# A hybrid two-layer block on one core: front, second norm, mixer's bias, first delta-rule head's preparation and end rewritten around unchanged heads

## The reference, cut to what matters

```
for i in range(2):
    shift, scale, gate = split(silu(c) @ ada_w[i] + ada_b[i])        # c_shift, c_scale, c_gate from c_ctx
    h  = rms_norm(x,   norm_w[i]) * (1 + scale)   + shift             # x: 256 latent tokens, ctx: 256 context tokens
    hc = rms_norm(ctx, norm_w[i]) * (1 + c_scale) + c_shift           # width 2048
    if i == 0:   # mixer: spatial gate  u * (w_s @ layernorm(v) + b_s) * silu(ga)  in 8 groups,
                 # and attention with 8 heads, 2 key/value heads, rms-normed and rotated q, k
        o, oc = ab_mixer(h, hc, ...)
    else:        # q, k, v through a 5-tap convolution and silu, 16 key heads x 2 value heads, gated delta rule
                 # in both directions (chunks), output rms-normed, times silu(z), then @ w_out
        o, oc = dn_mixer(h, hc, ...)          # only the latent part of the output is needed
    x = x + gate * o
    if i == 0: ctx = ctx + c_gate * oc
return rms_norm(x, final_norm_w)
```

## Time and profile before

| what | us |
|---|---|
| median of 3 runs (2880.4 to 2884.49) | 2881.23 |
| the profiled execution, its own time | 2878.12 |
| its span, first to last instruction | 2876.3 |
| PE busy in it (92%) | 2650.1 |
| DVE, ACT, POOL busy | 1219.5, 1233.4, 1287.2 |
| mean granted clock of TensorE, share of full speed | 0.964 |

### The profile page before, as it was taken

How to read it: one execution, slowest core, us unless ns; L and a number is a source line. 1 busy time by engine, 2 the same in 40 slices (tenths; PEclk the granted TensorE clock), 3 DMA queues, 4 the chain that set the end, 5 groups by cost and what they waited for, 6 DMA issues and landing times.

```text
span 2876.3 us, 58157 instructions
## 1 busy us (share of the span) xinstructions
PE 2650.1 (92%) x24892; PEld 2223.1 (77%) x24892; DVE 1219.5 (42%) x2427; ACT 1233.4 (43%) x2210; POOL 1287.2 (45%) x780
## 2 busy tenths in 40 slices
PE   4699999999999665999999999999999999997898
PEld 0277777777778454888888888888888888886897
DVE  0212222222310322565565555655655566554323
ACT  2422333333322324465456545654565456443333
POOL 2032333333245524544554555455545554551353
PEclk8899999999999877999999999999999999998999
DMA  6835444455442202213222322232222222214554
GB/s 277 330 108 185 186 174 174 183 190 190 161 176 88 73 30 91 74 61 104 89 76 67 104 82 82 68 101 85 78 71 97 89 74 75 97 53 147 183 184 132
DMA packets 98897, 351.54 MB, mean 122 GB/s; under 512 B 10833, under 2 KB 15313, under 8 KB 96210
## 3 DMA queue, kind: packets, MB, share of 16 engines
q1 hardware_dynamic: 98642, 347.82, 34.3%
HBM read 335.59 MB, written 12.19 MB: 121 GB/s over the span
## 4 chain that ended last, share of the span: by engine, by line
PE 72%; POOL 12%; issue 6%; DVE 3%; DMA 3%; ACT 3%; SPq 0%; POOLq 0%; ACTq 0%; DVEq 0%
PE bank L522 8%; PE bank L524 7%; PE bank L523 7%; PE bank L684 4%; PE bank L686 4%; PE bank L685 4%; POOL wl L385 3%; PE bank L790 3%; PE bank L498 3%; POOL scratch L2059 2%; DMA raw<-w_ada 2%; PE bank L724 2%; PE bank L808 2%; PE bank L726 2%; PE bank L725 2%
## 5 line engine op out<-in xcount | busy, mean ns | idle before, releaser
L385 POOL TENSOR_TENSOR wl<-raw,wh 128x1024 fp32r<-128x1024 f32 x210 | 500.3, 2386 | 722.3 <-ACT wh L380 722.3
L380 ACT ACTIVATE wh<-raw 128x1024 fp32r<-128x1024 f32 x226 | 238.7, 1059 | 548.5 <-PE bank L686 258.4
L684 PE MATMUL bank<-hh,wh 128*128 128x512 f32 (+1 forms) x1040 | 410.6, 395 | 49.7 <-POOL wl L385 24.8
L686 PE MATMUL bank<-hh,wl 128*128 128x512 f32 (+1 forms) x1040 | 387.4, 372 | 0.9 <-issue 0.9
L685 PE MATMUL bank<-hl,wh 128*128 128x512 f32 (+1 forms) x1040 | 385.8, 371 | 1.3 <-issue 1.3
L684 PEld LDWEIGHTS bank<-hh,wh 128*128 128x128 f32 x1040 | 201.7, 194 | 86.1 <-POOL wl L385 25.9
L522 PE MATMUL bank<-hh,wh 128*128 128x512 f32 x640 | 256.8, 401 | 11.8 <-POOL wl L328 11.8
L328 POOL TENSOR_TENSOR wl<-raw,wh 128x1024 fp32r<-128x1024 f32 x56 | 136.7, 2446 | 254.7 <-ACT wh L323 254.7
L524 PE MATMUL bank<-hh,wl 128*128 128x512 f32 x640 | 250.4, 391 | 0.0
L523 PE MATMUL bank<-hl,wh 128*128 128x512 f32 x640 | 250.2, 391 | 0.0
L686 PEld LDWEIGHTS bank<-hh,wl 128*128 128x128 f32 x1040 | 201.3, 194 | 35.9 <-issue 1.7
(11 more groups left out here) (277 smaller groups left out, 5995.6 us busy)
## 6 DMA issues: line engine op xcount, KB each, us to landing
raw<-w_in SPq DMA_DIRECT2D x258, 512.0 KB, 3.5
raw<-w_ada SPq DMA_DIRECT2D x124, 512.0 KB, 6.5
raw<-w_out SPq DMA_DIRECT2D x84, 512.0 KB, 3.8
scratch<-w_ada SPq DMA_DIRECT2D x68, 512.0 KB, 6.3
scratch<-keep_g SPq DMA_DIRECT2D x16, 1024.0 KB, 6.0
scratch<-w_in SPq DMA_DIRECT2D x24, 512.0 KB, 7.0
scratch<-xT SPq DMA_DIRECT2D x2, 4096.0 KB, 12.8
keep_y<-scratch SPq DMA_DIRECT2D x30, 256.0 KB, 2.4
```

The source lines that it names most:

```text
L380: eng.activation(buffers(s)[0], raw[:, s % RAW, :], ACT.Copy).then_inc(sem("rear_hi"), 1)
L385: eng.tensor_tensor(buffers(s)[1], raw[:, s % RAW, :], buffers(s)[0].bitcast(F32), ALU.subtract)\
L684: pe.matmul(ps, w[:, k * P:(k + 1) * P], hhv[:, kk, t0:t1], start=first and k == k0, stop=False)
L686: done = pe.matmul(ps, r[:, k * P:(k + 1) * P], hhv[:, kk, t0:t1], start=False, stop=last and k == k1 - 1)
```

## The change

Six parts; the numbers are used again further on.

1. Front: the squares 0 to 9 come ahead of the rows of block 0 and 10 to 15 behind them; `square_sum(0)` comes after three units of block 2; a read-out of rows stands behind every second `norm_affine`; the first halves of key tiles 0 and 1 are loaded after block 5 and multiplied inside blocks 6 and 7; half 2 is loaded after block 6, and its split stands behind `norm_affine(11)`.
2. Mixer: the bias is loaded on all partitions and added by DVE; the matmul of ones goes.
3. Second norm: eight buffers of each kind instead of two.
4. Head 0: sums of the decay rows come in the middle of the key tile, later weight halves are split between the steps, two of the four coupling tiles and both attention tiles go from POOL to DVE, the second value tile's convolution goes behind `turn_first`.
5. Last head: the first two output halves are multiplied in four quarters between steps of the scan, for which y of heads 0 to 7 must be back (counted on `g_kept`).
6. Last norm: the product with `final_w` is made on ACT beside the output tiles, the product with the root is shared by DVE (10 tiles) and POOL (6), and 8 stores of two tiles replace 16.

```
+SOONER = {5: (0, 1), 6: (2,)}
@@ order of the ring (front_places), and the same on SP
     for a in range(len(EARLY)):
         eighths(a, 0, 8)
-    for h in range(4 * KVH):
+        for h in SOONER.get(a, ()):
+            half(h)
+    for h in range(3, 4 * KVH):
         half(h)
+        def norm_t(layer, k):
+            return xres[:, k % 8, :] if layer else n_t[k % 2]
+        def norm_full(layer, k):
+            return xres[:, 8 + k % 8, :] if layer else n_full[k % 2]
@@ SP
-            sp.dma_start(sgub[0:1, :], sgu_b).then_inc(sem("mix_in"), 16)
+            sp.dma_start(sgub, sgu_b[0:1, :].to_broadcast([P, GROUPS * P])).then_inc(sem("mix_in"), 16)
...
+                back = sem("g_kept" if h < KH // 2 else "y_back")
...
@@ PE, front
-                ada(a, 3, 8, pb[2 + a % 2])
-                if a == 1:
+                if a == 2:
                     square_sum(0)
+                ada(a, 3, 5, pb[2 + a % 2])
+                if a >= NEARLY - 2:
+                    front_half(a - NEARLY + 2, pb[a - NEARLY + 2][:, :], True, False, "h_lo", 0)
+                ada(a, 5, 8, pb[2 + a % 2])
...
-            kv_tile(0)
-            kv_tile(1)
+            front_half(2, pb[0][:, :], False, True, "h_lo", 1)
+            front_half(3, pb[1][:, :], False, True, None, 1)
@@ PE, mixer
-                pe.matmul(pb[5][:, :].rearrange("p (t n) -> p t n", n=P), ones[0:1, :], rep, start=True, stop=False)
@@ PE, head 0 (k and q quarters stood ahead of the sums, turn_k, make_kk, make_kq behind both v tiles)
+            k_quarter(0, 0, pb[4])
+            k_quarter(0, 1, pb[4])
             pe.wait_ge(sem("g_ready"), 1)
...
+            k_quarter(0, 2, pb[4])
             pe.wait_ge(sem("gc_ready"), 1)
...
+            v_quarter(0, 0, 0, pb[6])
+            turn_k(0)
+            v_quarter(0, 0, 1, pb[6])
+            make_kk(0)
+            v_quarter(0, 0, 2, pb[6])
+            make_kq(0)
+            v_quarter(0, 0, 3, pb[6])
@@ PE, last head
                 scan_su(i, 1)
                 if more:
                     z_eighth(i, 1, PB)
+                else:
+                    out_quarter(0)
...
@@ ACT, head 0
             for t in range(NT):
                 decay_distance(0, t)
-            decay(0)
+                decay(0, t, t + 1)
+                if t == 0:
+                    rear_split_hi(act, 9)
+            rear_split_hi(act, 10)
@@ DVE, mixer
-                dve.tensor_tensor(xv[:, n, :], pb[5][:, :], a_ug, ALU.mult).then_inc(sem("a_merged"), 1)
+                ch.link(dve.tensor_tensor(xv[:, n, :].rearrange("p (t n) -> p t n", n=P),
+                                          pb[5][:, :].rearrange("p (t n) -> p t n", n=P), rep, ALU.add))
+                dve.tensor_tensor(xv[:, n, :], xv[:, n, :], a_ug, ALU.mult).then_inc(sem("a_merged"), 1)
@@ DVE, head 0 (new)
+            for t in (2, 3):
+                dve.wait_ge(sem("e_exp"), t + 1)
+                dve.tensor_tensor(q4(attn[0][t - 2]), q4(CT(0, t)), each_v(KQM[:, 2 * (t - 2) * P:2 * (t - 1) * P]),
+                                  ALU.mult).then_inc(sem("at_ready"), 1)
+                ch.link(dve.tensor_tensor(q4(CT(0, t)), q4(CT(0, t)), each_v(KKM[:, 2 * t * P:2 * (t + 1) * P]),
+                                          ALU.mult))
+                dve.tensor_tensor(u4(CT(0, t)), u4(CT(0, t)), coef(0, 0, t), ALU.mult).then_inc(sem("c_ready"), 1)
             for g in range(2):
                 turn_first(0, g)
+            conv_v(0, 1, pb[7], 0, 5)
@@ end
+                act.activation(f_out[:, t, :], x1[:, t, :], ACT.Copy, scale=smc("final_w")[:, t:t + 1])
-            for k in range(KT):
-                dve.scalar_tensor_tensor(out=f_out[:, k, :], in0=x1[:, k, :], scalar=smc("final_w")[:, k:k + 1],
-                                         in1=f_rinv, op0=ALU.mult, op1=ALU.mult).then_inc(sem("f_scaled"), 1)
+            for k in range(10):
+                dve.tensor_tensor(f_out[:, k, :], f_out[:, k, :], f_rinv, ALU.mult).then_inc(sem("f_scaled"), 1)
+            for k in range(10, KT):                                   # on POOL
+                pool.tensor_tensor(f_out[:, k, :], f_out[:, k, :], f_rinv, ALU.mult).then_inc(sem("n_added"), 1)
```

More of the change, by code:

```diff
@@ L482, in _, with store @@
                 rear_load(sp, s, w_out1[s - NDELTA, :, :])
-            for k in range(KT):
-                sp.wait_ge(sem("f_scaled"), k + 1)
-                sp.dma_start(out[k, :, :], f_out[:, k, :]).then_inc(sem("stored"), 16)
-            sp.wait_ge(sem("stored"), 16 * KT)
+            pairs = out.rearrange("k p t -> p k t")
+            def store(j):
+                sp.dma_start(pairs[:, 2 * j:2 * j + 2, :], f_out[:, 2 * j:2 * j + 2, :]).then_inc(sem("stored"), 16)
+            for j in range(5):
+                sp.wait_ge(sem("f_scaled"), 2 * j + 2)
+                store(j)
+                if j in (1, 2, 4):
+                    p = (1, 2, 4).index(j)
+                    sp.wait_ge(sem("n_added"), 3 * (KT - 1) + 2 * p + 2)
+                    store(5 + p)
+            sp.wait_ge(sem("stored"), 16 * KT // 2)
         @block.tensor
@@ L512, in square_sum, with front_half @@
                 pe.matmul(pb[6][:, :], ones[:, :], n_acc, start=True, stop=True).then_inc(sem("n_summed"), 1)
-            def front_half(h, ps, first, last, ready=None):
+            def front_half(h, ps, first, last, ready=None, part=None):
                 pe.wait_ge(sem("front_lo"), h + 1)
@@ L892, in scan_su, with out_quarter @@
                 done.then_inc(sem("su_made"), 1)
+            def out_quarter(q):
+                s = NDELTA + q // 2
+                if q == 0:
+                    pe.wait_ge(sem("z_silu"), KH)
+                    pe.wait_ge(sem("g_kept"), 16 * 2 * NT + 32 * (KH // 2))
+                if q % 2 == 0:
+                    wait_lo(pe, s)
+                w, r = buffers(s)
+                for k in range(4 * (q % 2), 4 * (q % 2) + 4):
+                    kk = (q // 2) * HALF + k
+                    ps = PA[:, 0:SEG]
+                    pe.matmul(ps, w[:, k * P:(k + 1) * P], hhy[:, kk, :], start=(kk == 0), stop=False)
+                    pe.matmul(ps, w[:, k * P:(k + 1) * P], hly[:, kk, :], start=False, stop=False)
+                    done = pe.matmul(ps, r[:, k * P:(k + 1) * P], hhy[:, kk, :], start=False, stop=False)
+                if q % 2:
+                    done.then_inc(sem("rear_done"), 1)
             def query_s(i, t):
@@ L917, in _ @@
             products(1, 0, HALF, PA[:, :], 0, T, False, True, "h_lo")
-            for q in range(4):
-                k_quarter(0, q, pb[4])
             pe.wait_ge(sem("ba_copied"), 1)
@@ L923, in _ @@
             done.then_inc(sem("ba_turned"), 1)
-            for q in range(4):
-                q_quarter(0, q, pb[5])
+            k_quarter(0, 0, pb[4])
+            k_quarter(0, 1, pb[4])
             pe.wait_ge(sem("g_ready"), 1)
@@ L933, in _ @@
             done.then_inc(sem("g_summed"), 1)
-            for q in range(4):
-                v_quarter(0, 0, q, pb[6])
+            k_quarter(0, 2, pb[4])
             pe.wait_ge(sem("gc_ready"), 1)
@@ L1063, in _ @@
                     pe.wait_ge(sem("x2_ready"), t - 1)
-                for j in range(4):
+                for j in range(2 if t == 0 else 0, 4):
                     s = NDELTA + 4 * t + j
@@ L1156, in k_root @@
                    .then_inc(sem("k_root"), 1)
-            for h in range(4):
-                front_split_hi(act, h)
+            front_split_hi(act, 4)
             kv_copy(0)
             k_square(0)
-            front_split_hi(act, 4)
             front_split_hi(act, 5)
@@ L1288, in _ @@
                .then_inc(sem("gexp"), 1)
[L1289 to L1294 removed]
+            rear_split_hi(act, 5)
             def decay_distance(h, t):
@@ L1303, in decay_distance, with decay @@
                 last.then_inc(sem("e_min"), 1)
-            def decay(h):
-                for t in range(NT):
+            def decay(h, t0=0, t1=NT):
+                for t in range(t0, t1):
                     act.wait_ge(sem("e_min"), 4 * h + t + 1)
@@ L1953, in _ @@
                 scan_s(i, 0)
+                if not more:
+                    rear_split_lo(dve, NDELTA + 1)
                 scan_r(i, 1)
@@ L2116, in _ @@
                 add_final(k)
+            pool.wait_ge(sem("n_scaled"), 2 * KT + 1)
+            for k in range(10, KT):
+                pool.tensor_tensor(f_out[:, k, :], f_out[:, k, :], f_rinv, ALU.mult).then_inc(sem("n_added"), 1)
 def halves(w):
@@ L2200 @@
     tiles0 = [32, 33, 34, 35] + [t for g in range(GROUPS) for t in (24 + g, 8 + g, g, 16 + g, 36 + g)]
-    h0 = h0[[2 * t + b for t in tiles0 for b in range(2)]]
+    order0 = [2 * t + b for t in tiles0 for b in range(2)]
+    order0[1:3] = order0[2:0:-1]
+    h0 = h0[order0]
     w1 = np.asarray(dn_w_in[0])
```

155 lines of the change are left out of this document (87 added, 68 removed).

## The result

| | us |
|---|---|
| before, median of 4 runs (2880.4 to 2884.49) | 2882.09 |
| changed, median of 4 runs (2789.84 to 2798.23) | 2794.07 |
| ratio, 95% interval | 0.9694, [0.9676, 0.9712] |
| the changed kernel's profiled execution: its time, its span | 2791.92, 2790.1 |
| predicted | 2793.0, range 2775 to 2811 |

The kernel is 88.0 us faster. That the total was met to 1 us says little yet, since it is a sum of six terms. The two profiled executions have spans 86.2 us apart, and seven instructions that stand in both cut them into eight stretches. The first two groups are rows of the changed kernel's timeline, one engine at a time (columns as in the earlier trace rows).

A forecast was written before the change was run, and what follows sets the result against it. PE was taken as the limit in mixer and heads, standing still in edited places; DVE and POOL limit the second norm. 33 + 8.4 + 1.5 + 49 - 4.7 + 1 = 88.2 us off 2881.23 gives 2793, range 2775 to 2811.

The forecast's parts named there:

- six slots hold 7.7 us of loads, so PE's absence alone costs DMA little: Front: an early half takes 6.2 us of PE, which the loads in six slots were to cover.
- single stall of half 2: Front: half 2's slot comes free only when split, behind two more norm tiles, putting the end of block 7 at 108.
- a sign of being wrong: Front: the prediction is wrong if the first norm's ACT queue holds back the ring for longer than one half.
- Rival (a): Second norm: DVE and POOL run free of the lock, 14 us off instead of 1.5, total 2780; chance 0.13.
- the 3 kept back: Head 0: 3 us kept from 51.8 for unseen waits, POOL's two first subtractions and ACT's wait for the late convolution.
- POOL's two subtractions as late work: Head 0: POOL now begins with two subtractions, 4.8 us, that used to be done, covered by the 3 us kept.
- the clock should rise earlier: ... less 0.9 for one step: Last scan: one step at the upper clock, 1.13 against 2.08 us, takes 0.9 us off the quarters' cost.
- rival (c): Last scan: filled gaps keep the clock up, five slow steps gain 4.7 us, cancelling part 5, total 2788; chance 0.12.
- 7.6 us at worst: Last products: POOL's six at 0.6 us and DVE's ten at 0.4, one after the other.
- Rival (d): Heads: another rhythm after head 0 starts with POOL and ACT behind, needing 5.9 us a head; chance 0.02.
- longer than 1442 / 15 = 96 us each: Heads: the prediction is wrong if the heads take longer than 96 us each.
- Rival (b): Front and head 0: lower clock, ring starves twice, 25 instead of 33 and 42 instead of 49, total 2808; chance 0.22.

The follow-up runs named there:

- the experiment: Changed kernel with the four output quarters put back behind the last head's scan, early loads of y kept: 2790.28 us, ratio 0.9697.
- three edits: Changed kernel with second norm's low part, head 0's first_inverse (POOL's two subtractions behind the masks) and all 16 last products on DVE: 2777.74 us, ratio 0.965.

## Why the prediction was right, point by point

**Part 1**, 33 predicted, 30.2 in the profile. The stall went as forecast: `square_sum(0)` stands at 41.38 (predicted 41) and waits for nothing. `ada_sum(7)` came at 114.6, not 109, and the copy at 133.1, not 129. The step that failed is "six slots hold 7.7 us of loads, so PE's absence alone costs DMA little", with its single stall of half 2: the DMA rate is down by a third from 80 us on. SP's queue stood 6.4 us on PE's first early half, as well as the 7.1 us on half 2 that I had foreseen, and 5.6 us on the low parts of halves 0 and 1, which the sum leaves out. (The 7.1 us are also a little more than a half's 6.2, the length that I had named as a sign of being wrong; the front stayed within its bounds of 25 and 38.) Part of the miss is no step at all: the same front ended between 129.0 and 135.9 us in ten runs, 131.7 in the mean, which makes the term about 32 against the one profile of the kernel before. The profile of the table is one of the two among those ten in which the clock fell ahead of the first early half (0.66 and 0.54 between 80 and 95 us, 0.89 in the others).

**Part 2**, 8.4 predicted, 9.4 measured, 811.9 against 801.6 us with the one matmul put back. The mechanism held, and DVE's second operation is hidden. The size was off: a group is 75.04 - 73.80 = 1.24 us shorter, more than the 1.12 us that the row covers, where I had taken 1.05; the stretch lies just above my bound of 9.

**Part 3**, 1.5 predicted, 3.5 measured, within its bounds of 0 and 14. The limit was named rightly. The period is 5.90 us for three tiles, 1.97 a tile, where I had stepped through to 2.1 and wrote that it stays above that. In this pattern POOL works off two tiles, then one, and DVE fits one scaling of 0.68 us between without meeting it. Rival (a), 14 us, is refuted; taking POOL out altogether gives 6.5 us more.

**Part 4**, 49 predicted, 46.3 measured. From the copy to the first matmul of `base(0, 0)` it is 63.2 us, against the 62.2 that I used (59.2 and the 3 kept back). Of the 4.0 above 59.2, `first_inverse` began 2.3 late (54.75, not 52.4), and from there to PE's start it took 8.4 us instead of 6.8. The rest lies behind it: the second group of `base(0, 0)` waited 1.36 us for a mask. One step failed at both places: I had counted POOL's two subtractions as late work, not as a lock on the masks, and beside them the masks take 2.07 and 2.10 us instead of 0.42. Undoing that, with the inverse on DVE, gave 4.1 us.

**Part 5**, 4.7 lost predicted, 0.8 measured between the two profiles and 1.5 in the experiment. The step that failed is "the clock should rise earlier: ... less 0.9 for one step". It rose halfway through the first quarter, so the other quarters ran at 0.28 us a matmul, and three steps, not one, went from about 2 us to 1.05. This is rival (c), to which I gave 0.12, and it is right in its mechanism: the slow steps that lie ahead of the first quarter were, as (c) allowed, not reached. The size of 0.8 is luck. In eight of the eleven profiles with quarters the clock rose only behind the first one, and the stretch lost 2.2 to 2.4 us, about half of the forecast and half of what (c) would have given back.

**Part 6**, 1 predicted, -0.4 measured, below my bound of 0. That the two engines would take turns was foreseen, 7.6 us at worst, and they took 6.6. But the last store, of two tiles, ends 2.8 us behind its issue (2781.06 + 6.23 = 2787.29, span 2790.1), where the last of one tile took 1.8 (2866.82 + 7.72 = 2874.54, span 2876.3). I had left that out.

**The heads**, 0 predicted, 1.8 lost. Rival (d), another rhythm, does occur but at 0.1 us a head and not 5.9; it is told below. My sign "longer than 1442 / 15 = 96 us each" was no sign: a head without a stop takes 96.3 to 96.6 us in both kernels, so it would have fired with nothing changed. Rival (b) holds in part: the ring starves more than once, and the front and head 0 together gave 5.5 us less than forecast, of the 15 that it asked for.

So the mechanisms named were right in the main and the range had room, but the total met to 1 us is luck: terms off by up to 3.9 us, in both directions, nearly cancelled.

## What to carry to other kernels

Giving POOL a share of DVE's work can cost time where the two exclude each other: DVE alone was faster at both places (33.3 against 39.8 us, 5.45 against 6.60), and POOL's own late work held DVE's masks up (2.07 us against 0.42). Taking work from POOL for DVE still gained 2.3 us in head 0. Matmuls that fill gaps in a chain of short steps can pay for part of themselves through the clock; how much depends on when it rises, so one profile does not settle it. And a total that is met to 1 us can hide terms that are off by 4: check it by stretches.

## What the runs showed that I had not expected

PE stops in the heads behind nothing but its own issue. In the timeline of the changed kernel's PE the first of more than 0.6 us is this one, and seven like it follow, six of them each some 194 us (two heads) behind the last:

```profile
1235.47 0.26 PE L812 MATMUL bank<-scratch 32*32 32x32 f32 x7 [1.52 <-issue]
```

That is 197.7 us behind the start of `base(0, 0)`; when the same kernel ran again it was 198.1. In the changed kernel heads with a stop took 97.5 to 98.1 us, the others but the first 96.4. Eight stops add to 9.2 us up to the last head's first `scan_vn`, where the kernel before had seven of 8.2 in the same stretch, the first 221.4 us behind its `base(0, 0)`, others at 415 and 610. That is 1.0 of the 1.8 us that the heads lost. With the ones matmuls put back, the first stop moved to 30.9 us and the next ones to 224.6, 418.5 and 612.1, close to those of the kernel before:

```profile
1077.87 0.50 PE L709 MATMUL bank<-hl,wh 128*128 128x512 f32 x1 [1.79 <-issue]
```

In seven of the eight profiles with edits on other engines alone it stayed at 198 to 199; in the eighth, of three edits, there is none above 0.6 us there, and the first is at 390.4. So their place depends on what stands in PE's own list, far ahead of them, and an edit in the mixer can cost or save a microsecond or two in loops that it does not touch.

The profile points at a cause. It has a DMA queue of kind "instruction", with 198 packets of 16 KB, 149 of them in the 1507 us of the heads. From 1232.5 to 1233 us, just ahead of the stop shown first, it has one:

```profile
q8 instruction: 1, 0.02, 16.8%
```

The thirteen profiles hold 89 stops of more than 0.6 us in the heads, at several places of the loop. Every one of them begins once a packet of this queue has begun, and ends 2.2 to 2.8 us after the packet's start. Most packets come without a stop. That PE stands there until its next instructions have arrived fits all of this, but no run here varied the supply of instructions. Four profiles also have one stop of 2.1 to 2.4 us outside the pattern, once in the changed kernel's second profile where its first has none, so not every stop is the program's.
